# Summing the squares of two RMS norms by adding transfers instead of GpSimd adds, in a one-layer encoder step

## The reference

```python
h = x + 0.5 * swiglu(rmsnorm(x, g_ffn1), w1g, w1u, w1d)        # norm 0
u = rmsnorm(h, g_mix)                                          # norm 1
h = h + concat(attention_A(u), attention_B(u)) @ w_out
h = h + 0.5 * swiglu(rmsnorm(h, g_ffn2), w2g, w2u, w2d)        # norm 2
y = rmsnorm(h, final_norm)                                     # norm 3

def rmsnorm(x, g): return x * rsqrt(mean(x * x, axis=-1) + 1e-6) * g
def swiglu(x, wg, wu, wd): return (silu(x @ wg) * (x @ wu)) @ wd
```

## Time and profile before

| | |
|---|---|
| median of three executions | 1045.59 us (1044.27 to 1046.47) |
| the profiled execution | 1045.55 us, its span 1043.7 us |
| PE busy | 1025.3 us, 98% of the span |
| DVE busy | 804.3 us, 77% |
| ACT busy | 562.9 us, 54% |
| POOL busy | 167.8 us, 16% |

### The profile page before, as it was taken

The page is one execution under the profiler, slowest core; times in us unless marked ns, Lnnn a source line. Parts: engine busy times, 40 slices in busy tenths (PEclk is TensorE's granted clock), DMA queues, the critical chain, the costliest instruction groups (busy, mean ns, idle before and its releaser), DMA issues. The chain is left out here.

```text
span 1043.7 us, 19555 instructions
## 1 busy us (share of the span) xinstructions
PE 1025.3 (98%) x7620; PEld 1001.1 (96%) x7620; DVE 804.3 (77%) x1253; ACT 562.9 (54%) x968; POOL 167.8 (16%) x296
## 2 busy tenths in 40 slices
PE   9999999999999999999999999999999999999996
PEld 9999999999999999989889889999999999999995
DVE  6998777888678895368767866798877878867895
ACT  7546554666456663344435544644555566546664
POOL 0000000000010035223455202200000000000023
PEclk9999999999999999999999999999999999999998
DMA  5426666655665446230112212415666665666542
GB/s 207 130 84 160 171 163 166 188 151 154 182 170 150 130 120 210 61 96 22 51 52 72 76 42 81 122 41 158 173 174 149 157 190 149 159 188 173 129 120 91
DMA packets 38890, 137.33 MB, mean 132 GB/s; under 512 B 5456, under 2 KB 8656, under 8 KB 38672
## 3 DMA queue, kind: packets, MB, share of 16 engines
q1 hardware_dynamic: 30736, 107.52, 30.0%
q0 software_dynamic: 8064, 28.58, 17.2%
HBM read 131.10 MB, written 4.98 MB: 130 GB/s over the span
## 5 line engine op out<-in xcount | busy, mean ns | idle before, releaser
L1776 DVE TENSOR_TENSOR w_lo<-raw,w_hi 128x1024 fp32r<-128x1024 f32 (+4 forms) x187 | 198.8, 1065 | 109.8 <-ACT w_hi L1282 94.1
L944 PE MATMUL acc<-c_hi,w_lo 128*128 128x288 f32 x952 | 282.0, 296 | 0.0
L944 PE MATMUL acc<-c_hi,w_hi 128*128 128x288 f32 x952 | 280.9, 295 | 0.0
L944 PE MATMUL acc<-c_lo,w_hi 128*128 128x288 f32 x952 | 277.6, 292 | 0.0
L1282 ACT ACTIVATE w_hi<-raw 128x1024 fp32r<-128x1024 f32 (+4 forms) x157 | 140.6, 897 | 79.8 <-PE acc L944 56.8
L1438 ACT ACTIVATE comb<-acc 128x288 f32<-128x288 f32 x224 | 92.2, 411 | 167.0 <-PE acc L944 164.8
L944 PEld LDWEIGHTS acc<-c_lo,w_hi 128*128 128x128 f32 x952 | 180.8, 190 | 0.0
L944 PEld LDWEIGHTS acc<-c_hi,w_hi 128*128 128x128 f32 x952 | 179.0, 188 | 0.0
L944 PEld LDWEIGHTS acc<-c_hi,w_lo 128*128 128x128 f32 x952 | 178.5, 188 | 0.0
L944 PE MATMUL acc<-h_hi,w_hi 128*128 128x288 f32 x574 | 170.8, 298 | 1.9 <-ACT comb L1438 0.8
L944 PE MATMUL acc<-h_hi,w_lo 128*128 128x288 f32 x574 | 169.8, 296 | 0.0
(11 more groups left out here) (253 smaller groups left out, 1841.8 us busy)
## 6 DMA issues: line engine op xcount, KB each, us to landing
raw<-in_w1st SPq DMA_DIRECT2D x17, 768.0 KB, 4.3
raw<-in_w2st SPq DMA_DIRECT2D x17, 768.0 KB, 4.2
raw<-in_w_qk SPq DMA_DIRECT2D x13, 512.0 KB, 3.8
raw<-in_w1sd SPq DMA_DIRECT2D x8, 768.0 KB, 4.4
raw<-in_w2sd SPq DMA_DIRECT2D x8, 768.0 KB, 4.2
raw<-in_w1gu SPq DMA_DIRECT2D x10, 512.0 KB, 4.6
raw<-in_w2gu SPq DMA_DIRECT2D x10, 512.0 KB, 3.8
raw<-in_w1st SPq DMA_DIRECT2D x9, 512.0 KB, 5.1
```

What stands on the lines that cost most here:

```text
L944: m = nc.tensor.matmul(acc[:, banks[side_of(p)], 0:HALF], w_part[:, col:col + P], x_part, start=n in (P1, P5, P2) and k == 0 and e == 0, s ...
L1776: return nc.vector.tensor_tensor(cols, src, hi.bitcast(FP32), ALU.subtract).then_inc(split_ready, 1)
```

## The change

In `sums`, the first five squares (i = 0 to 4, KD - 3) of norms 1 and 3 are no longer added by POOL's `tensor_tensor`, but by a transfer that POOL issues, from `sq` or `h_even` onto `ssq`, with the add done on the way. The rest stay POOL adds. A new semaphore, `ssq_summed`, counts the transfers, and all that waited for the n-th add now does so through `wait_added`. The order of the waits is the same: transfer n is issued only once transfer n-1 has landed, and a square is written only once its buffer's former tile is in.

In `late_period`, ACT's copies of products (`snap`) move ahead of `next_hi` and `next_square`: the copy of P1 ahead of `next_hi(done[0])`, that of P5 ahead of `next_square(done[0])`, that of P6 ahead of `next_hi(done[-1])`; and `next_square(done[-1])` moves behind the rounding of the next weights (`hi_a1`, or `hi_block(("qk", 0))`), ahead of the copy of P7.

```diff
+        def wait_added(engine, norm, n):
+
+            if 0 < n <= SUM_DMAS[norm]:
+                engine.wait_ge(ssq_summed, 16 * (DMAS_BEFORE[norm] + n))
+            else:
+                engine.wait_ge(ssq_added, ADDS_BEFORE[norm] + max(n - SUM_DMAS[norm], 0))
...
                 if p == BRIDGE:
                     hi_down(ffn_no, KD - 1, 0)
                     hi_down(ffn_no, KD - 1, 1)
-                elif ffn_no == 0:
+                snap(snap_g[:, p % 2, 0, :], ffn_no, p, P1)
+                if p > BRIDGE and ffn_no == 0:
                     next_hi(ffn_no, done[0])
-                snap(snap_g[:, p % 2, 0, :], ffn_no, p, P1)
+                snap(snap_u[:, 1, :], ffn_no, p, P5)
                 if p > BRIDGE:
                     next_square(ffn_no, done[0])
-                snap(snap_u[:, 1, :], ffn_no, p, P5)
+                snap(snap_g[:, p % 2, 1, :], ffn_no, p, P6)
                 if ffn_no == 0:
                     next_hi(ffn_no, done[-1])
-                snap(snap_g[:, p % 2, 1, :], ffn_no, p, P6)
-                next_square(ffn_no, done[-1])
                 if not last:
                     hi_a1(ffn_no, p + 1)
                 elif ffn_no == 0:
                     hi_block(("qk", 0))
+                next_square(ffn_no, done[-1])
                 snap(snap_u[:, 0, :], ffn_no, p, P7)
...
                 for d in range(KD - 1 if norm == 3 else KD):
                     gp.wait_ge(sq_ready, KD * norm + d + 1)
-                    gp.wait_ge(ssq_added, KD * norm + d)
+                    wait_added(gp, norm, d)
                     square = h_even if norm != 2 and d % 2 else sq
-                    nc.gpsimd.tensor_tensor(ssq[:], ssq[:], square, ALU.add).then_inc(ssq_added, 1)
+                    if d < SUM_DMAS[norm]:
+                        nc.gpsimd.dma_start(ssq[:], square, accum_op=ALU.add).then_inc(ssq_summed, 16)
+                    else:
+                        nc.gpsimd.tensor_tensor(ssq[:], ssq[:], square, ALU.add).then_inc(ssq_added, 1)
...
+SUM_DMAS = (0, KD - 3, 0, KD - 3)
+ADDS_BEFORE = (0, KD, KD + 3, 2 * KD + 3)
+DMAS_BEFORE = (0, 0, KD - 3, KD - 3)
```

More of the change, by code:

```diff
@@ L504, in hybrid_step @@
         ssq_added = sem("ssq_added")
+        ssq_summed = sem("ssq_summed")
         uhi_ready = sem("uhi_ready")
@@ L853, in token_sums @@
             def token_sums(norm, bank):
-                pe.wait_ge(ssq_added, KD * (norm + 1))
+                wait_added(pe, norm, KD)
                 for tt in range(TOK_TILES):
@@ L1012, in final_sums @@
                     wait_sds(1)
-                    pe.wait_ge(ssq_added, KD * 4 - 1)
+                    wait_added(pe, 3, KD - 1)
                 tok = slice(t * HALF, (t + 1) * HALF)
@@ L1533, in residual_next @@
                 act.wait_ge(res_ready, count + d + 1)
-                act.wait_ge(ssq_added, KD * norm + d)
+                wait_added(act, norm, d)
                 u_hi_part(norm, d)
@@ L1563, in next_square @@
                 else:
-                    act.wait_ge(ssq_added, KD * norm + i - 1)
+                    wait_added(act, norm, i - 1)
                 nc.scalar.activation((sq, h_even)[i % 2], res[:, ORDER[i], :], ACT.Square).then_inc(sq_ready, 1)
```

## The result

| | before | after |
|---|---|---|
| median on the same chip, 4 runs each | 1044.93 us (1044.11 to 1046.47) | 1055.37 us (1053.40 to 1057.82) |
| ratio, 95% interval | | 1.0104 (1.0092 to 1.0116) |
| profiled execution | 1045.55 us | 1056.08 us, span 1054.3 |

The forecast was 1049.9 us, range 1045.0 to 1054.0. The direction was right and the size was not: the measured median lies 1.4 us above the range.

The account below looks back on a forecast made before the run. PE, busy 98% of the span, was taken as the bound, with about 0.4 us of slack at `final_sums(0)`. From 1045.55 us, less 0.7 (first feed-forward), plus 5.1 (tail), came 1049.95, stated as 1049.9 us, range 1045.0 to 1054.0.

Parts of the forecast that it names:

- The gaps behind ACT's copies: First feed-forward: PE's gaps of 0.59 and 0.57 us before P7 and P6 go, together 1.16 us.
- DVE no longer stretched: Second feed-forward: without POOL's adds the 128x384 remainder takes 0.55 instead of 1.79 us; PE gaps of 0.61 us should go.
- The price of a link: Each 288 KB adding transfer of the chains: 1.5 us to start, 2.0 moving, 0.8 landing, so 4.3 us.
- The tail: End of second feed-forward: fifth transfer lands at 1033.6, square 6 and `final_sums(0)` come 5.1 us later, swallowing PE's 0.61.
- The first feed-forward: First feed-forward: fifth transfer lands at 393.9, `token_sums` gains at best 1.4 us, at worst nothing; 0.7 us gain taken.
- The queue behind squares 2 and 4: Late periods: P7's copy waits behind these squares; covered in the second feed-forward, may cost some tenths in the first.
- the removed 1.16 and 0.21: First feed-forward: PE gaps of 1.16 us before P7 and P6, and 0.21 us wait of `token_sums` for POOL's last add.
- Quick transfers: Rival for both chains: a link at 2.6 us, deciding from 3.3 us downwards, squares set the pace, 1043.6 us; chance 0.12.
- Transfers slower than the weights': Rival for both chains: links above 4.5 us; at 4.9, end 8.2 and `token_sums` 1.4 us late, 1055.2 us; chance 0.16.

Follow-up runs that it names:

- e1: Kernel after with no adding transfers, only the new order of ACT's work, POOL adding all squares: 1045.27 us, 1.0013 against the kernel before.
- e2: Kernel after with the change in `late_period` undone, so the transfers with ACT's old order: 1049.74 us, 1.0054 against the kernel before.
- e3: Kernel after with the five transfers for norm 1 alone, new order kept: 1050.44 us, 1.0055 against the kernel before.
- e10: e4 with 36 useless matmuls put before PE's wait in `final_sums`: 1050.57 us, 1.0057 against the kernel before.
- e9: e5 with SP's loads held until the fifth transfer of norm 1 has landed: 1057.31 us, 1.0114 against the kernel before.
- e5: Kernel after with squares 2 and 4 of the late periods moved behind ACT's copy of P7: 1062.21 us, 1.0162 against the kernel before.
- e6: Kernel after with three projection weight loads beside norm 1's transfers cut to 64 KB each: 1055.38 us, 1.0094 against the kernel before.
- e7: Kernel after with its transfers copying instead of adding, so sums hold the last tiles alone: 1042.96 us, 0.9977 against the kernel before.
- e12: Kernel before with `next_hi` behind copies of P1 and P6, two transfers for norm 3 alone, its squares 2 and 4 behind P7's copy: 1043.41 us, 0.9994.
- e4: Kernel after with the five transfers for norm 3 alone, new order kept: 1050.78 us, 1.0061 against the kernel before.

## Why the prediction was right in direction and wrong in size

- **The gaps behind ACT's copies (-1.16 us).** Gone as forecast, but the saving shows nowhere as time: in e1 POOL's adds took it back through DVE, in the kernel after the waits before P4 did.
- **DVE no longer stretched.** Right: `w_lo` of 128x384 at 1016.34 takes 0.55 us, 1.79 in the earlier trace rows.
- **The price of a link, 4.3 us: nearly right, and in part by luck.** The DMA view gives 4.3 as the median landing of ten, but slow and quick ones are mixed in it. Undisturbed a link is 4.0: 3.5 us to the landing, of which 1.7 are moving by the queue's share (2.0 in the working) and 1.8 are start and landing (2.3; its 0.8 for the landing was too much, since the earlier trace rows has the last packets 0.4 us before it), and 0.5 us from the landing to the next issue, which the working left out. (The line of the earlier trace rows is that of 928 to 934 us; 940 to 946 has 57.1%, which gives the same 3.4 us.)
- **The tail, +5.1 us: the mechanism right, the size helped by luck.** The fifth transfer lands when square 6 starts, at 1038.46; less the 4.56 us carried in it is 1033.9, where 1033.6 was forecast. `final_sums` comes 1041.57 - 4.56 - 1031.76 = 5.25 us late. Links of 4.0 from 1021.03 on would have landed it nearly 2 us sooner; the second link of 5.7 made up for that. In e2, where that link was 4.3, the stretch lost 4.9 instead of 6.0. Of the slow link (1021.03) the DMA view shows one late stretch on few of the DMA engines beside an instruction packet. In the second link of each chain such a packet stands in the view also where the link was 4.2 (e2) or 4.6 us (e3), so it does not settle the length by itself; the cause is open. What was missed is the lower clock after PE's idle time: from `final_sums` to the end of the span it is 12.7 us instead of 11.9, the remaining 0.8 us, which is also what e10 gives back in its trace.
- **The first feed-forward, -0.7 us: the step that failed.** It measured +4.6, so two terms were mis-sized. The first is the landing of the fifth transfer: the working took the second chain, moved it by 640.2 us and added 0.5 us for SP's loads, 393.9; it landed at 397.75. By ACT's and POOL's rows the chain fell behind that shifted one by 1.2 us in the first link and 1.1 in the third, both beside SP's loads, by 1.9 in the second, and by 0.2 in the last two together. That loads do this is shown by e9 against e5 (3.5 instead of 8.4 us), and how much depends on when they are issued: 7.6 and 8.0 us for the third link where transfer and load start together (e5, e3), 5.5 here, where the loads were 1.5 us ahead. The second link has no large load beside it, and its 1.9 us stay open.
- **The queue behind squares 2 and 4, "some tenths": the other term of that step.** It was 1.18 + 2.95 = 4.1 us of PE's time, plus what the lower clock costs behind it (some 1.4 us by the spacing of the matmuls up to 393.35), plus a wait of 0.6 us for `u_lo`, less the removed 1.16 and 0.21: 4.8 where the stretch lost 4.6. The place was found; its price was taken from the second feed-forward, where the late end covers it, and not worked out for a late third transfer (landing 388.96, by the working 385.3). e5 shows the queue as the cause of these waits, and shows too that curing it alone is worse.
- **Adding the parts.** Order alone +1.2, sums alone +5.6, both +10.4. Why the links are longer in the new order (e2 against the kernel after) is not shown, nor why e6's median stayed where it was.
- **The rivals.** "Quick transfers" was wrong for an adding transfer and right as a mechanism: e7. "Transfers slower than the weights'" named 1055.2 us, and 1055.4 was measured; that is chance. It wanted links of 4.9 us throughout and an end 8.2 us late; undisturbed links were 4.0 and the end 5.25 us late, and the rest was lost in the first feed-forward before P4.

## What to carry to other kernels

A chain of small adding transfers cost about 4 us for each link of 288 KB even with an idle queue, against 1.4 to 1.8 us for the GpSimd add it replaces. Five such links lost 4.9 to 6.6 us at the end, where all the rest waits for them, and in the first feed-forward anything from 0.6 to 12.3 us, by what stood beside and behind them; two, with slack behind them (e12), did no harm and perhaps gained a little. When a step becomes a wait for a transfer, go through everything that stands behind it in its engine's own list, and price it with the transfer late. A time taken from the same place of another stage holds only if the loads beside it are the same and the same work covers it, and a faster engine may bring those loads forward into the transfer. What a stretch lost is read between two fixed places of the same trace, not from the time at which it ends (e6).

## What the hardware showed that was not expected

- The add doubles the moving: 1.7 us of each DMA engine for 288 KB against 0.8 us plain. POOL's issue of it takes 0.86 against 0.54 us.
- An adding transfer beside SP's loads took 8.4 us where it took 3.5 with the loads held (e5, e9).
- After 2.8 us of idle time PE's granted clock was 0.58 over the next 3.9 us, and after 4.6 us (e4) 0.50 over the next 4.0; work of no use in that time kept it at 1.00 (e10).
- A 128x768 remainder of DVE took 2.19 us under one POOL add (1.94 us) and 0.95 alone (e1).
